# Where a decoder trunk's weight casts sit in its first stages, and a last stage that starts without a barrier

## The reference, cut to what matters

```python
# layer 0: gMLP mixer, dense SwiGLU, per-layer embedding
x = x + gmlp_mixer(rms_norm(x, mix_norm_g[0]), ...)
x = x + swiglu(rms_norm(x, ffn_norm_g[0]), w_gate, w_up, w_down)        # 2816 wide
x = x + (p[0] @ w_proj[0]) * sigmoid(rms_norm(x, ple_norm_g[0]) @ w_gate[0])
# layer 1: sliding-window attention against one shared K/V, top 2 of 8 experts, embedding
x = x + swa_sink_attention(...)
hn = rms_norm(x, ffn_norm_g[1])
x = x + sum_e combine[:, e:e+1] * swiglu(hn, moe_w_gate[e], moe_w_up[e], moe_w_down[e])   # 3584 wide
x = x + (p[1] @ w_proj[1]) * sigmoid(rms_norm(x, ple_norm_g[1]) @ w_gate[1])
return rms_norm(x, final_norm_g)
```

## Time and profile before

| | us |
|---|---|
| runs | 4335.07, 4339.06, 4602.17; median 4339.06 |
| profiled execution | 4306.77, its span 4305.2 (core 6, the slowest) |
| other cores' spans | 4209.3 to 4303.0 |
| dense SwiGLU, 837 to 1409 | 572 |
| PLE0, 1409 to 1597 | 188 |
| attention, 1597 to 2122 | 525 |
| last stage, 4029 to 4305 | 276 |

### The profile page before, as it was taken

The page is one execution under the profiler, slowest core; times in us unless marked ns, Lnnn a source line. Parts: engine busy times, 40 slices in busy tenths (PEclk is TensorE's granted clock), DMA queues, the critical chain, the costliest instruction groups (busy, mean ns, idle before and its releaser), DMA issues.

```text
span 4305.2 us, 68531 instructions; the slowest of 8 cores (4209.3 to 4305.2 us)
## 1 busy us (share of the span) xinstructions
PE 3491.6 (81%) x20783; PEld 1990.8 (46%) x21030; DVE 1257.3 (29%) x2477; ACT 1030.7 (24%) x2319; POOL 588.5 (14%) x588
## 2 busy tenths in 40 slices
PE   4888848798899546755757999999999999999445
PEld 2555533354456323433653545546464646464222
DVE  2544531122222336745531111111111111111153
ACT  2555520011211322332421111111111111111133
POOL 1111122200000222221011000000010101010132
PEclk8999979899999777877858999999999999999767
DMA  9578769656655995999629897969696969795631
GB/s 158 89 117 129 108 134 229 179 84 97 100 86 91 195 177 80 112 109 109 106 110 259 201 241 172 255 163 265 170 264 173 254 185 255 196 239 141 203 124 59
DMA packets 368662, 691.02 MB, mean 161 GB/s; under 512 B 21642, under 2 KB 289708, under 8 KB 353836
## 3 DMA queue, kind: packets, MB, share of 16 engines
q0 software_dynamic: 280384, 299.40, 49.7%
q1 hardware_dynamic: 69772, 345.26, 24.0%
q10 hardware_dynamic: 18144, 41.95, 2.7%
HBM read 866.00 MB, written 212.21 MB: 250 GB/s over the span
## 4 chain that ended last, share of the span: by engine, by line
PE 71%; DMA 10%; issue 8%; DVE 5%; ACT 3%; POOL 2%; another core or an unknown queue 1%; DVEq 0%; SPq 0%; ACTq 0%; POOLq 0%
PE ps L247 68%; PE ps L250 3%; DMA arena<-xs 3%; DVE arena L270 2%; ACT arena L258 2%; DMA arena<-wgu 2%; DVE arena L261 1%; DMA arena<-gmlp_w_in 1%; ACT L258 1%; DMA xs<-arena 1%; DMA arena<-gmlp_w_out 1%; DMA arena<-ygs,arena 1%; POOL xgs L1354 1%; DMA arena<-gmlp_w_s 1%; POOL arena L291 1%
## 5 line engine op out<-in xcount | busy, mean ns | idle before, releaser
L247 PE MATMUL ps<-arena 128*128 128x512 bf16 (+7 forms) x18889 | 3321.9, 337 | 254.7 <-ACT arena L258 68.3
L247 PEld LDWEIGHTS ps<-arena 128*128 128x128 bf16 (+2 forms) x19136 | 1834.6, 103 | 1703.1 <-issue 454.8
L258 ACT ACTIVATE arena<-ps 128x512 f32<-128x512 f32 (+3 forms) x720 | 369.9, 516 | 1524.0 <-PE ps L247 1501.6
L261 DVE TENSOR_TENSOR arena<-arena,ps 128x512 bf16<-128x512 f32 (+3 forms) x619 | 351.3, 569 | 1239.3 <-PE ps L247 1140.1
L250 PE MATMUL ps<-arena 128*128 128x128 bf16 (+2 forms) x1894 | 210.7, 261 | 540.6 <-DVE arena L270 128.1
L250 PEld LDWEIGHTS ps<-arena 128*128 128x128 bf16 (+2 forms) x1894 | 165.2, 123 | 592.4 <-issue 583.1
L261 POOL TENSOR_TENSOR arena<-arena 128x512 f32<-128x512 f32 (+4 forms) x196 | 263.4, 1356 | 770.2 <-DVE arena L270 356.5
L258 ACT ACTIVATE arena<-arena 128x512 bf16<-128x512 bf16 (+9 forms) x300 | 193.6, 648 | 550.6 <-DMA arena<-xs 360.3
L1439 POOL DMA_DIRECT2D arena<-wdn x120 | 110.5, 925 | 1497.2 <-PE ps L247 1492.6
L275 ACT COPY arena<-ps 128x512 f32<-128x512 f32 (+1 forms) x166 | 134.1, 808 | 752.5 <-PE ps L247 588.3
L277 DVE COPY arena<-ps 128x512 f32<-128x512 f32 (+4 forms) x179 | 101.3, 569 | 696.6 <-PE ps L247 588.8
(11 more groups left out here) (38 smaller groups left out, 280.6 us busy)
## 6 DMA issues: line engine op xcount, KB each, us to landing
arena<-wgu SPq DMA_DIRECT2D x105, 2048.0 KB, 11.7
arena<-wdn POOLq DMA_DIRECT2D x120, 896.0 KB, 26.6
wgu<-moe_w_gate POOLq DMA_DIRECT2D x56, 1024.0 KB, 20.1
wgu<-moe_w_up POOLq DMA_DIRECT2D x56, 1024.0 KB, 24.4
ygs<-arena ACTq DMA_DIRECT2D x92, 256.0 KB, 6.4
arena<-xc SPq DMA_DIRECT2D x34, 512.0 KB, 11.1
xs<-arena ACTq DMA_DIRECT2D x34, 512.0 KB, 8.0
arena<-xs SPq DMA_DIRECT2D x34, 512.0 KB, 11.9
```

What stands on the lines that cost most here:

```text
L247: P.add("pe", lambda h: h.matmul(out, lhsT, rhs, start=start, stop=stop), reads=r, writes=w)
L258: P.add("act", lambda h: h.activation(out=out, in_=in_, func=func, scale=scale, **kw), reads=r, writes=w)
L261: P.add(eng, lambda h: h.tensor_tensor(out=out, in0=in0, in1=in1, op=op), reads=r, writes=w)
```

## The change

It does six things.

- gMLP: a cast behind every third v group instead of every fourth: 34 casts instead of 27.
- Dense SwiGLU: a cast behind every third f instead of every sixth, in the same tiles: seven per tile instead of three, with the three at the blocks' ends as before: 43 instead of 27.
- PLE0: none instead of 12. Attention: its places are unchanged, so it now takes the last 35 instead of 46, and its last places are empty.
- The zero fill moves from PLE0 to the dense stage: 46 DMAs of 256 KB on SP, named at even f of tiles 1 to 4. Its tile is cleared on DVE.
- The last stage's weights (`tail_weights`) are issued ahead of the last slot's `gate_up`; its rows and first eight embedding inputs (`tail_rows`) behind it, into memory that the gate/up weights and expert inputs have left. There is no barrier: the gathers wait for the stores of `yg_d` themselves. Rows no longer travel with the gathers.
- The last stage's blocks run in a software pipeline: block k's gate beside the transposes of k+1, the norm of k+2 and the combine of k+6; the square of k comes one block later; roots are taken for four blocks at a time, at k = 1, 5, 9, 13, 15. Before, blocks went in groups of 2, 2, 4, 4, 4 with all of a group's roots and outputs at its end.

```diff
@@ -587,7 +587,7 @@
             v_group(t, blk, j)
             for _ in range(-(-len(mixq) // (len(vq) - n))):
                 mix_group(*mixq.pop(0))
-            if 0 < t < NG - 1 and n % 4 == 3:
+            if 0 < t < NG - 1 and n % 3 == 2:
                 PP.issue(1, [("vg", p, j, blk)])
...
+    zt = alloc([128, D], BF16)
+    MS("dve", zt, 0.0, ["zt"])
+    nz = [0]
...
-            if f % 6 == 5 and t > 0 and t + 1 < NFT:
+            if t > 0 and f % 2 == 0 and nz[0] < NROW:
+                DMA("sp", xg_d[nz[0]:nz[0] + 128, :], zt, "xst", ["zt"], [("xz", nz[0])])
+                nz[0] += 128
+            if f % 3 == 2 and t > 0 and t + 1 < NFT:
                 PP.issue(1, [("act", f - 1)])
...
-    zt = alloc([128, 2 * D], BF16)
-    MS("pool", zt, 0.0, ["zt"])
...
-        for _ in range(2):
-            if nz[0] < NROW:
-                n0 = nz[0]
-                nn = min(256, NROW - n0)
-                DMA("sp", xg_d[n0:n0 + nn, :].rearrange("(p a) d -> p (a d)", p=128), zt[:, 0:nn * D // 128], "xst", ["zt"], [("xz", n0)])
-                nz[0] += nn
-        if 2 <= n < 14:
-            PP.issue(1, [("tm", 1)])
...
+    state["off"] = o_gw
+    xr = [alloc([128, D], F32) for _ in range(12)]
...
+    state["off"] = o_ht
+    xr += [alloc([128, D], F32) for _ in range(4)]
...
+    def xbuf_keys(j):
+        if j < 12:
+            return [("gw", j // 4)]
+        return [("hTe", (j - 12) // 2, b) for b in range(4)]
+
+    def t_pin(j):
+        DMA("sp", pin[j % 8], p1_in[j * 128:(j + 1) * 128, :], "tp%d" % (j % 8), [], [("pin", j % 8)] + (["xgt"] if j < 8 else []))
+
+    def tail_weights():
+        DMA("sp", gbp, W["ple_norm_g"][1].partition_broadcast(128), "dc", [], ["gbp"])
+        DMA("sp", gbf, W["final_norm_g"].partition_broadcast(128), "dc", [], ["gbf"])
+        DMA("pool", wgt, W["ple_w_gate"][1].rearrange("(k p) n -> p k n", p=128), "wa0", [], ["wgt"])
+        DMA("pool", wpj, W["ple_w_proj"][1].rearrange("(k p) n -> p k n", p=128), "wa1", [], ["wpj"])
+        MS("dve", sN, 0.0, [("sN", j) for j in range(16)])
+        MS("dve", sF, 0.0, [("sF", j) for j in range(16)])
+
+    def tail_rows():
+        for j in range(16):
+            DMA("sp", xr[j], xr_d[j * 128:(j + 1) * 128, :], "tx%d" % j, [("xr_d", j)], [("xr", j)] + xbuf_keys(j))
+        for j in range(8):
+            t_pin(j)
...
+        if n == NS - 1:
+            tail_weights()
         gate_up(n)
+        if n == NS - 1:
+            tail_rows()
         down(n)
-    epoch()
...
-    groups = [[0, 1], [2, 3], [4, 5, 6, 7], [8, 9, 10, 11], [12, 13, 14, 15], [], []]
-
-    def t_load(j):
-        DMA("sp", xr[j], xr_d[j * 128:(j + 1) * 128, :], "xld%d" % (j % 3), [("xr_d", j), ("xld", j % 3)], [("xr", j), ("xld", j % 3)])
-        DMA("sp", pin[j % 8], p1_in[j * 128:(j + 1) * 128, :], ("dx", "dx2", "dp", "wr2")[j % 4], [], [("pin", j % 8)])
...
+    def t_gath(j):
         for a_, (t_, nm, sm) in enumerate(((ya, "ya", "ga"), (yb, "yb", "gb"))):
             P.add("pool", lambda h, t_=t_, a_=a_: h.indirect_dma_start(
                 out=t_[j % 4], out_offset=None, in_=yg_d,
                 in_offset=bass.IndirectOffsetOnAxis(ap=posi[:, a_, j:j + 1], axis=0)),
-                reads=[], writes=[(nm, j % 4)], dma_sem="%s%d" % (sm, j % 4))
+                reads=YGK, writes=[(nm, j % 4)], dma_sem="%s%d" % (sm, j % 4))
+
+    YGK = [("yg_d", s_, hf, b) for s_ in range(NS) for hf in range(2) for b in range(SLOT_W[s_] // 128)]
...
-            t_load(j + 4)
-
-    def t_rs(s_, nm, js):
-        if not js:
+            t_gath(j + 4)
+    def t_rs(pairs):
+        pairs = [(s_, nm, js) for s_, nm, js in pairs if js]
+        for s_, nm, js in pairs:
+            sv = s_[:, js[0]:js[-1] + 1]
+            kk = [(nm, j) for j in js]
+            TS("dve", sv, sv, 1.0 / D, ALU.mult, kk, kk, s2=EPS, op1=ALU.add)
+        for s_, nm, js in pairs:
+            sv = s_[:, js[0]:js[-1] + 1]
+            kk = [(nm, j) for j in js]
+            ACT(sv, sv, AF.Sqrt, kk, kk)
+        for s_, nm, js in pairs:
+            sv = s_[:, js[0]:js[-1] + 1]
+            kk = [(nm, j) for j in js]
+            RECIP(sv, sv, kk, kk)
...
+        if j + 8 < NB:
+            t_pin(j + 8)
...
-        ACT(junk, x_, AF.Square, [("xh", j, 0), ("xh", j, 1), ("sF", j)], ["junk", ("sF", j)], accum=sF[:, j:j + 1])
+
+    def t_sq(j):
+        ACT(junk, xr[j], AF.Square, [("xh", j, 0), ("xh", j, 1), ("sF", j)], ["junk", ("sF", j)], accum=sF[:, j:j + 1])
...
-    for g in range(5):
-        n = len(groups[g])
-        for i, j in enumerate(groups[g]):
-            for j2 in share(groups[g + 1], i, n):
-                t_norm1(j2)
-            for j2 in share(groups[g + 1], i, n):
-                t_norm2(j2)
-            t_gate(j)
-            for j2 in share(groups[g + 2], i, n):
-                t_comb(j2)
-        t_rs(sF, "sF", groups[g])
-        t_rs(sN, "sN", groups[g + 2])
-        for j in groups[g]:
-            t_out(j)
+        t_gath(j)
+    t_comb(0)
+    t_comb(1)
+    t_rs([(sN, "sN", [0, 1])])
+    t_norm1(0)
+    t_norm2(0)
+    t_norm1(1)
+    t_comb(2)
+    t_comb(3)
+    t_rs([(sN, "sN", [2, 3])])
+    ready = []
+    for k in range(NB):
+        t_norm2(k + 1)
+        t_norm1(k + 2)
+        t_gate(k)
+        for j in ([4, 5, 6] if k == 0 else [k + 6]):
+            if j < NB:
+                t_comb(j)
+        if k > 0:
+            t_sq(k - 1)
+        if k in (1, 5, 9, 13, 15):
+            js = list(range(13 if k == 15 else max(0, k - 4), k))
+            t_rs(([(sN, "sN", list(range(k + 3, k + 7)))] if k < 10 else []) + [(sF, "sF", js)])
+            ready += js
+        for _ in range(2 if len(ready) > 3 else 1):
+            if ready:
+                t_out(ready.pop(0))
+    t_sq(NB - 1)
+    t_rs([(sF, "sF", [15])])
+    for j in ready + [15]:
+        t_out(j)
```

More of the change, by code:

```diff
@@ L765, in build @@
         f_load(t + 2)
+    assert nz[0] >= NROW
     barrier_keep(WGK + WPK, skip=("pl",))
@@ L875, in build @@
     pend = []
-    nz = [0]
     for n, b in enumerate(order):
@@ L1379, in build @@
     epoch()
+    o_gw = state["off"]
     gwt = [alloc([128, 8, 1024], BF16) for _ in range(3)]
+    o_dw = state["off"]
     dwt = [alloc([128, 28, 512], BF16) for _ in range(2)]
+    o_ac = state["off"]
     actE = alloc([128, 28, 512], BF16)
+    o_ht = state["off"]
     hTe = [alloc([128, 8, 512], BF16) for _ in range(2)]
+    o_xg = state["off"]
     xgt = alloc([128, 4, D], BF16)
@@ L1502, in down @@
             issue_dw()
+    o_free = state["off"]
+    wgt = alloc([128, 8, D], BF16)
+    wpj = alloc([128, 2, D], BF16)
+    gbp = alloc([128, D], F32)
+    gbf = alloc([128, D], F32)
+    sN = alloc([128, 16], F32)
+    sF = alloc([128, 16], F32)
+    assert state["off"] <= ARENA_B - 1024
+    state["off"] = o_gw
+    xr = [alloc([128, D], F32) for _ in range(12)]
+    assert state["off"] <= o_dw
+    ya = [alloc([128, D], F32) for _ in range(4)]
+    yb = [alloc([128, D], F32) for _ in range(4)]
+    hb = [alloc([128, D], BF16) for _ in range(3)]
+    hTb = [alloc([128, 8, 128], BF16) for _ in range(6)]
+    pTb = [alloc([128, 2, 128], BF16) for _ in range(6)]
+    assert state["off"] <= o_ac
+    state["off"] = o_ac
+    gs = [alloc([128, 512], F32) for _ in range(2)]
+    tm = [alloc([128, 512], F32) for _ in range(2)]
+    yo = [alloc([128, D], F32) for _ in range(2)]
+    junk = alloc([128, D], BF16)
+    state["off"] = o_ht
+    xr += [alloc([128, D], F32) for _ in range(4)]
+    assert state["off"] <= o_xg
+    pin = [alloc([128, PLE], F32) for _ in range(8)]
+    def xbuf_keys(j):
[16 more added lines that the diff above has]
+            t_pin(j)
     issue_xg(0)
@@ L1550, in t_load @@
                 in_offset=bass.IndirectOffsetOnAxis(ap=posi[:, a_, j:j + 1], axis=0)),
-                reads=[], writes=[(nm, j % 4)], dma_sem="%s%d" % (sm, j % 4))
+                reads=YGK, writes=[(nm, j % 4)], dma_sem="%s%d" % (sm, j % 4))
+    YGK = [("yg_d", s_, hf, b) for s_ in range(NS) for hf in range(2) for b in range(SLOT_W[s_] // 128)]
+    outs = []
+    NB = 16
     def t_comb(j):
@@ L1559, in t_comb, with t_norm1 @@
         if j + 4 < NB:
-            t_load(j + 4)
-    def t_rs(s_, nm, js):
-        if not js:
-            return
-        sv = s_[:, js[0]:js[-1] + 1]
-        kk = [(nm, j) for j in js]
-        TS("dve", sv, sv, 1.0 / D, ALU.mult, kk, kk, s2=EPS, op1=ALU.add)
-        ACT(sv, sv, AF.Sqrt, kk, kk)
-        RECIP(sv, sv, kk, kk)
-    def t_norm1(j):
+            t_gath(j + 4)
[13 more added lines that the diff above has]
+            RECIP(sv, sv, kk, kk)
+    def t_norm1(j):
+        if j >= NB:
+            return
         STT("dve", hb[j % 3], xr[j], sN[:, j:j + 1], gbp, ALU.mult, ALU.mult, [("xr", j), ("sN", j), "gbp"], [("hb", j % 3)])
     def t_norm2(j):
+        if j >= NB:
+            return
         bk = 4 + j % 2
```

39 lines of the change are left out of this document (removed).

## The result

The changed kernel takes 4232 us in the median of its runs against 4339 before: a ratio of **0.9753** (95% interval 0.9724 to 0.9781), 107 us less. The forecast was 169 less. Now and then all cores of a die run some per cent slower, whatever the kernel; ratios and stage times here leave such executions and cores out. The profiled execution of the change took 4234.65 us; its slowest core is core 3 (span 4233.0), not core 6 as before. So I compare stage by stage, with the profiled executions of both kernels (the barriers' memsets and the last `ygs` store are the borders; us): the mean over the eight cores, and in the fifth column the difference on cores 1, 3, 5 and 6 alone, the four late ones of before. The forecast was read from core 6, one of these four, so it answers to that column.

What follows compares the result with a forecast made beforehand. No engine bounded the touched stages end to end; only the dense stage was near its engine, PE. Terms 49 + 8 + 33 + 100 − 3 − 15 − 3 = 169, and 4339 − 169 = 4170 us; range 4115 to 4245.

Steps and rivals of the forecast that it cites:

- PLE0's weights: PLE0: its weights are issued on POOL behind the last casts; cost 3 us (0 to 25).
- 91 us are the casts': Attention before: of ACT's 129.4 us in four waits, 91 were put down to POOL standing before casts.
- Last stage, 100: Last stage: early rows and weights, no barrier and the pipeline take it from 276 to 176 us; gain 100 (75 to 120).
- The slow chain of rows: Rival, last stage: each row link takes 13.6 us instead of about 5, taking the stage's gain whole; 4270, chance 0.03.
- not 40: Rival, last stage: DVE and POOL slow each other at 32 adds, costing 40 us; 4210, chance 0.12.
- PLE0, 49: PLE0 without casts and zero fill: blocks run at 5.86 us, ending near 1548 instead of 1597; gain 49 us.
- Dense stage, 15: Dense stage: added casts and zero fill make the next tile's loads land later; cost 15 us (0 to 74).
- the saturated case: Rival, dense stage: loads land in 29.5 us against 11.0, costing 74, and PLE0's weights come 25 late; 4250, chance 0.15.
- Attention, 33 and 8: Attention: two cast blocks instead of three gain 33 us (15 to 50); its start without a backlog gains 8 (0 to 12).
- the count decides: Attention: POOL's blocks follow the program's cast count, fourteen apart, so the new stage stands at its 9th and 23rd casts.
- gMLP, 3: gMLP: seven more casts, for which only block loads wait; cost 3 us (0 to 6).

Runs made afterwards that it cites:

- the freed POOL: Changed kernel with the dense stage's last seven casts left to attention and attention's elementwise POOL work moved to DVE; ratio to before 0.9584.

## Why the prediction was right or wrong, point by point

The direction and the last stage were right. On the late cores, from which the forecast was read, 70 of its 169 did not come, and four terms of the sum failed: PLE0's weights (25 of the 70), the expert slots, which the sum put at nothing without a reason (21), attention's "91 us are the casts'" (13) and the dense stage (11).

*Last stage, 100:* right, 95, and so was its mechanism: DVE 111.6 of work became 120.9, the first combine came at 7.3 where I let it take 7. The two parts were 28 and 67 instead of 24 and 76. The slow chain of rows did not occur (3.9 a link in the median and 5.2 at most, where its rival needed 13.6). In the tighter pipeline DVE and POOL both get slower: an add takes 1.69 instead of 1.585, a DVE operation of the combine 1.61 instead of 1.44; that is 12 us of work, not 40.

*PLE0, 49, with "PLE0's weights: cost 3 (0 to 25)":* the step that failed is the second. Its blocks run as said, but the weights land after 84 us and PE stands 22 to 28 for them on seven cores: the far end of my own range and past it. The 3 had no working beside it; it fits the queue of before, where these weights landed in 13.8, and not one that I was about to fill with sixteen more casts. With the queue thinned PLE0 is 140.

*Dense stage, 15:* the term was mis-sized, 31 measured (26 on the late cores). The mechanism is the one named: the last block load of three tiles lands 3 to 8 us later, and PE's waits grow by 19 on core 3. Left out were the stores at the end behind a full queue (7) and at most 4 for PE's clock after each wait. Of the saturated case's 74 it is less than half.

*Attention, 33 and 8:* the count decides, as I said: the long waits stand at the 58th, 72nd and 100th cast, in step with 72, 86 and 100 before. But one block in the stage, not two: the 86th cast went out at once. Why is open. A short queue is not the reason, since four or five casts were in flight there, and before the 72nd stood 27 us with four. One block less should have made the gain larger, and it was smaller, 18 (28 on the late cores): the step "91 us are the casts'" took ACT's waits for the delay. On core 3 the iterations show a delay of 66 before and 50 after, 16 less. The 8 for the stage's start was right: 6 on that core, 6 to 12 on all. An engine that is waited for at one place has its idle time there whether or not the others would have been slower anyway.

*gMLP, 3:* right in the mean, 0 on the late cores.

*What was missing:* the expert slots, 39 (21 on the late cores, 58 on those that led). No term and no rival of mine had them, because nothing is changed in fourteen of the fifteen. Before, the two cores of a pair entered the slots 44 to 51 us apart. Half of that came in attention, which took one 501 to 505 and the other 522 to 525, and 10 to 13 in PLE0; with casts re-placed both take 484 to 502 for attention and enter the slots 8 to 19 apart. There both fetch 2 MB pieces and down weights at the same moments. About 26 of the 39 come with casts and fill alone. The last stage's part alone makes the later cores 13 longer; its own cost inside the 39 is not separated from the spacing.

What is not settled: why the casts of before part the cores of a pair (the leader is not always the same core), which would need a run with the start of one core held back, and which casts of the count stand. Neither was tried.

So the forecast named the right direction and the largest term, but over a third of its gain did not come: a gain sized by waits instead of by delay, one load priced by the queue it would no longer find, a cost sized too low, and an effect on slots that the change doesn't touch.

## What to carry to other kernels

Transfers moved into a stage with idle DMA time are paid by what is issued last on the same queue, not by the median: price each late load by the queue that the change leaves, and keep the end of a stage thin (PLE0's weights paid it here, and in the freed POOL the router's). To size a blocked engine, line up the same iteration with and without the block; the sum of waits overstates it (66 for 88 here). An engine that issues long queues of software DMAs should do nothing that others wait for: that alone took attention from 504 to 438. Where two cores share memory, a stage's time depends on how far apart they arrive; compare pairs, not only the slowest core. And hold a forecast that was read from one core against the same kind of core, not against the mean of all.

## What the runs showed of the hardware

- POOL's long waits before a 1024 x 512 cast stood fourteen casts apart, counted over the program: before at the 72nd, 86th and 100th, after at the 58th, 72nd and 100th. Each lasts until one earlier cast is left in flight (on core 3 after: 47.6, 76.9 and 65.8 us). Not every such cast stands: after, the 86th went out at once with four in flight.
- Cores of a pair that start the expert slots 8 to 19 us apart take 1764 to 1793 us for them; 44 to 51 apart, the first takes 1713 to 1721 and the other 1751 to 1759. With half of the gate and up fetches taken away, all take 1718 to 1728 though 5 to 27 apart.
- In waits of 8.5, 10.6 and 9.1 us PE's granted clock fell from 1.00 to 0.50; over the 25 us behind them it was 0.92, 0.90 and 0.93.
